# Key products of a gated recurrence computed on GpSimd instead of VectorE

## The reference, cut to what matters

```python
def hgrn2_chunked(q, log_f, v):
    ...
    def step(state, inp):
        qt, lf, vt = inp
        kt = -jnp.expm1(lf)
        cum = jnp.cumsum(lf, axis=2)
        diff = cum[:, :, :, None, :] - cum[:, :, None, :, :]
        decay = jnp.exp(jnp.where(causal[:, :, None], diff, -jnp.inf))
        attn = jnp.einsum('bhtd,bhsd,bhtsd->bhts', qt, kt, decay)
        o = attn @ vt + jnp.einsum('bhtd,bhde->bhte', qt * jnp.exp(cum), state)
        last = cum[:, :, -1:, :]
        state = jnp.exp(last[:, :, 0, :, None]) * state + jnp.einsum('bhsd,bhse->bhde', kt * jnp.exp(last - cum), vt)
        return state, o
```

## Time and profile before

| quantity | value |
|---|---|
| median of 3 runs | 4072.37 us (4066.07 to 4079.21) |
| profiled execution, its own time | 4077.13 us |
| its span in the trace | 4075.4 us |
| busy TensorE / VectorE / ScalarE | 3347.7 / 1556.2 / 897.1 us |
| busy GpSimd | 0.2 us |
| levels' loop, layer 0 | first decayed product at 317.0 us, last gather from 361.28 us |
| levels' loop, layer 1 | first decayed product at 1249.8 us, last gather from 1294.09 us |

### The profile page before, as it was taken

One profiled execution on the slowest core, in us unless ns is written; L12 is line 12 of the kernel. 1 busy time (PEld: TensorE's weight loads), 2 busy tenths in 40 slices (PEclk: granted clock), 3 DMA queues, 4 the chain that ended last, 5 costly groups with the idle time before them and its releaser, 6 DMA issues. The chain is left out here.

```text
span 4075.4 us, 38108 instructions
## 1 busy us (share of the span) xinstructions
PE 3347.7 (82%) x16560; PEld 2233.5 (55%) x16560; DVE 1556.2 (38%) x1877; ACT 897.1 (22%) x1359; POOL 0.2 (0%) x4
## 2 busy tenths in 40 slices
PE   5986779999886779998998756668788885888887
PEld 3665757886665766886455536554333353433332
DVE  3536626653636636662003445622111225211212
ACT  3433223223433213232104410120000021000001
POOL 0000000000000000000000000000000000000000
PEclk9995979999996879999998976779999997899999
DMA  6270012322262002322110390019989750798885
GB/s 219 83 245 25 1 31 87 100 83 81 77 204 86 1 31 73 96 96 94 52 62 11 103 310 1 29 56 391 391 325 378 306 187 21 275 386 355 342 346 213
DMA packets 321109, 637.04 MB, mean 156 GB/s; under 512 B 12848, under 2 KB 208432, under 8 KB 320816
## 3 DMA queue, kind: packets, MB, share of 16 engines
q1 hardware_dynamic: 317856, 627.22, 42.5%
q10 hardware_dynamic: 3088, 7.40, 0.5%
HBM read 632.48 MB, written 2.10 MB: 156 GB/s over the span
## 5 line engine op out<-in xcount | busy, mean ns | idle before, releaser
L524 PE MATMUL ps<-ring,work 128*64 128x512 f32 (+1 forms) x3584 | 583.3, 548 | 195.6 <-DMA ring<-in_w_mod 59.1
L524 PE MATMUL ps<-mix_halves,work_halves 128*128 128x512 f32 (+1 forms) x1456 | 587.7, 404 | 30.1 <-DVE h_halves L1779 30.0
L524 PE MATMUL ps<-h_halves,work_halves 128*128 128x512 f32 (+1 forms) x1456 | 574.4, 395 | 34.5 <-DVE mix_halves L1779 34.5
L524 PEld LDWEIGHTS ps<-ring,work 128*64 128x64 f32 (+1 forms) x3584 | 221.9, 137 | 544.1 <-issue 526.8
L524 PE MATMUL ps<-mix_halves,ring_halves 128*128 128x512 f32 x1264 | 495.7, 392 | 0.0
L1779 DVE TENSOR_TENSOR ring_halves<-ring,work_halves 128x2048 fp32r<-128x2048 f32 x108 | 239.1, 2214 | 320.2 <-ACT work_halves L1266 319.4
L524 PEld LDWEIGHTS ps<-mix_halves,work_halves 128*128 128x128 f32 (+1 forms) x1456 | 276.0, 190 | 111.8 <-issue 31.6
L524 PEld LDWEIGHTS ps<-h_halves,work_halves 128*128 128x128 f32 (+1 forms) x1456 | 276.8, 190 | 100.5 <-issue 43.6
L1266 ACT ACTIVATE work_halves<-ring 128x2048 fp32r<-128x2048 f32 x108 | 199.7, 1849 | 487.9 <-PE ps L524 391.7
L524 PEld LDWEIGHTS ps<-mix_halves,ring_halves 128*128 128x128 f32 x1264 | 238.2, 188 | 52.5
L524 PE MATMUL ps<-ring,proj 128*64 128x512 f32 x1024 | 237.6, 624 | 17.9 <-ACT proj L1637 15.6
(11 more groups left out here) (352 smaller groups left out, 3767.3 us busy)
## 6 DMA issues: line engine op xcount, KB each, us to landing
ring<-in_w_exp_gate SPq DMA_DIRECT2D x128, 1024.0 KB, 8.5
ring<-in_w_exp_up SPq DMA_DIRECT2D x128, 1024.0 KB, 13.0
ring<-in_w_exp_down SPq DMA_DIRECT2D x128, 1024.0 KB, 11.6
ring<-in_ada_w SPq DMA_DIRECT2D x48, 1024.0 KB, 11.0
ring<-in_w_mod SPq DMA_DIRECT2D x48, 1024.0 KB, 11.0
ring<-in_w_in SPq DMA_DIRECT2D x22, 1024.0 KB, 5.2
ring<-in_w_gate SPq DMA_DIRECT2D x22, 1024.0 KB, 5.4
ring<-in_w_up SPq DMA_DIRECT2D x22, 1024.0 KB, 5.3
```

Of the source, the lines that this page charges most:

```text
L524: i = pe.matmul(o, lhsT, rhs, start=start, stop=stop, **kw)
```

## The change

The product of k with `b_e` leaves VectorE's program. GpSimd gets a program: for every level of both layers it waits for `b_decay`, from level 3 on also for `b_score` (TensorE has read the buffer that it will overwrite), writes k times `b_e` to `b_k[n % 2]`, and gives the new signal `b_kk`. TensorE waits for `b_kk` beside `b_qk` before the scores of levels 1 to 7. ScalarE waits for `b_kk` before it starts on the next distances, since its exponential overwrites `b_e`, and once more behind the seven levels. VectorE's `b_qk` now comes from the query product alone. The texts of the signals' table are adapted.

```diff
@@ -760,6 +760,8 @@
                 chunk_turns(proj[:, 10:12, :], 2, 4, "b_v")
                 for n in range(len(LEVELS) + 1):
                     pe.wait_ge(*due("b_qk"))
+                    if n:
+                        pe.wait_ge(*due("b_kk"))
                     if n == 1:
                         pe.wait_ge(*due("b_v_sb"))
                     for hd in range(H1):
@@ -1436,9 +1438,12 @@
                 to("b_v_sb", f(b_vt, ps[:, 4:6, :].rearrange("p b (c f) -> p (b c) f", c=2), ACT.Copy))
                 for n in range(len(LEVELS)):
                     act.wait_ge(*due("b_diff"))
+                    if n:
+                        act.wait_ge(*due("b_kk"))
                     link(f(b_d, b_d, ACT.Abs))
                     to("b_decay", f(b_e, b_d, ACT.Exp, scale=-1.0))
                 act.wait_ge(*due("b_qd"))
+                act.wait_ge(*due("b_kk"))
                 link(f(b_e, b_cum, ACT.Exp))
                 to("b_decay", f(b_d, b_d, ACT.Exp, scale=-1.0))
                 link(f(stats[:, 32:40].rearrange("p (b c) -> p b c", b=2),
@@ -1721,6 +1726,19 @@
             act.wait_ge(sem["stored"], 16)
 
 
+        @block.gpsimd
+        def _(pool):
+            due = Due(sem)
+            for l in range(2):
+                due("b_score", H1)
+                for n in range(1, len(LEVELS) + 1):
+                    pool.wait_ge(*due("b_decay"))
+                    if n >= 3:
+                        pool.wait_ge(*due("b_score", H1))
+                    pool.tensor_tensor(b_k[n % 2], proj[:, 8:10, :], b_e, ALU.mult).then_inc(sem["b_kk"], 1)
+                due("b_decay")
+                due("b_score", 2 * H1)
+
         @block.vector
         def _(dve):
             due = Due(sem)
@@ -1933,8 +1951,7 @@
                 difference(LEVELS[0])
                 for n in range(1, len(LEVELS) + 1):
                     dve.wait_ge(*due("b_decay"))
-                    tt(b_q[n % 2], q, b_e, ALU.mult)
-                    to("b_qk", tt(b_k[n % 2], z, b_e, ALU.mult))
+                    to("b_qk", tt(b_q[n % 2], q, b_e, ALU.mult))
                     dve.wait_ge(*due("b_qk", 2 if n == 1 else 1))
                     if n < len(LEVELS):
                         difference(LEVELS[n])
```

More of the change, by code:

```diff
@@ L220 @@
     "b_z": "VectorE: clamped logits", "b_ez": "ScalarE: exp(-z)", "b_f": "VectorE: forget gates", "b_lf": "ScalarE: their logs",
-    "b_qk": "VectorE: a level's q and k", "b_score": "TensorE: a head's scores", "b_acc": "VectorE: taken where they hold",
+    "b_qk": "VectorE: a level's q", "b_kk": "GpSimd: a level's k", "b_score": "TensorE: a head's scores", "b_acc": "VectorE: taken where they hold",
     "b_diff": "VectorE: distance to the level's middle", "b_decay": "ScalarE: its decay", "b_qd": "VectorE: distance to the chunk's end",
```

## The result

The changed kernel takes 4090.36 us (median of 13 runs, 4081.0 to 4095.22) where the kernel before, run beside it, takes 4076.28 (13 runs, 4066.07 to 4080.71). The ratio is 1.0034 with a 95% interval of 1.0024 to 1.0043, so +14 us with bounds of about +10 and +18. 4090 was forecast.

The account below looks back on a forecast made before the run. VectorE was taken to set the pace, 6.13 us a level. Twelve periods at +1.28 us (+15.4) and two last levels (+2.6) sum to +18.0; from the median 4072.37 the forecast is 4090 us, range 4058 to 4108.

Parts of the forecast that it names:

- Taking turns: VectorE's two-SBUF-input products and GpSimd's key product can't overlap: level 7.41 us, +18.0 in all; chance 0.57.
- together: Opposite case at the levels' start: both engines' products run at the same time, level about 5.15 us, sum -11.7.
- the marks named in advance: Profile signs in the levels: late or stretched distances (about 3.7 us), level 7.4 us, gathers 0.72, VectorE idle or stretched.
- that sum: A level's period: query product 1.23, GpSimd 2.45, to the gather 1.14, to the next level 2.59; 7.41 us.
- The term for G: Duration of GpSimd's 128x1024 key product, not in the earlier trace: taken as 2.45 us, bounds 1.22 and 6.55.
- Together and fast: First rival: both products overlap in the levels, GpSimd's under 3.7 us; 4060.7 us; chance 0.26 for under 3.
- Together with a slow GpSimd: Second rival: products overlap, but ScalarE's loop sets the pace; 4066 to 4079 us, at most 4112; chance within a shared 0.08.
- Turns with a slow GpSimd: Third rival: no overlap in the levels and GpSimd's product at 3.3 us, +30, 4102 us; chance 0.09 for over 3.
- No real change: Fourth rival: TensorE's start doesn't move, GpSimd's product at 1.22 us, +0.7 in all; chance within a shared 0.08.
- the cheaper order: In a level, distances slip in before GpSimd's product: +1.01 us a period, +14.7 in all.

Follow-up runs that it names:

- the query from PSUM: Changed kernel, but from level 2 on VectorE's query product reads a PSUM bank in place of q; 4078.5 us, one run (kernel before: 4070.91).
- the product beside the gather: Changed kernel, but GpSimd starts its key product only after query product and distances, ScalarE waiting before its exponential; 4076.24 us, ratio to before 1.0005.

## Why the prediction was right, and where it was off

**The mechanism.** Taking turns was the step that decided the sign, and it came out. From rows it was chosen against "together" by one comparison, 692 ns for a one-input operation and 1218 for a two-input one, read as VectorE having no read capacity left over for GpSimd. The comparison doesn't carry that, and the trace of the kernel before had the rows against it:

```profile
L2392 DVE TENSOR_TENSOR work<-proj,ps 128x1024 f32<-128x1024 f32 x16 | 19.5, 1221 | 186.5 <-PE ps L524 186.5
...
L1840 DVE TENSOR_REDUCE small<-h 128x4 f32<-128x1024 f32 x16 | 19.5, 1220 | 0.5
```

A product with only one input in SBUF takes 1221 ns and a reduction of a single input 1220, the same as two SBUF inputs. So a row's length doesn't tell how many read paths it takes, and as far as the sign rested on this comparison it was luck. What shows it are the runs: VectorE stretched with two SBUF inputs, not with one, and not against a write.

Of the marks named in advance, these came out: gathers at 0.72, a level over 6.13, TensorE late in the last level, and a stretched VectorE row with no idle time. Which row was named wrongly: the distances were to wait or to be stretched to 3.7 us; it was the query product, at 3.16, in six levels of seven, and the distances, at 3.25, in the first alone. The level was to be 7.4 us and is 6.93.

**The size.** A level was put at 7.41 us and is 6.93, so +0.80 where +1.28 was forecast. Three terms of that sum were off. GpSimd's product takes 2.34 us and not 2.45 (0.11). GpSimd starts at the decay while VectorE is still in its gather, so 0.27 us of its time lie beside work that doesn't collide; I let it start behind the query product, though the earlier trace rows had the room, 0.33 us between the exponential's end and VectorE's. And a product that has been held ends 1.08 us after the release, where I had put 1.23 for it (0.15). Together 0.53, less 0.05 for the steps between rows that the sum had left out: 0.48. That the order of the two hardly matters, as I wrote, is right to 0.1 us: the first level, where VectorE went ahead, costs 0.88 (6.93 against 6.05). For twelve levels (the first two of a layer cost 0.9 each) and the two last ones (+0.82 and +0.14 instead of +1.29 each; in layer 1 TensorE's last scores took 4.39 us instead of 5.13, at a mean granted clock of 0.78 from 1300 to 1310 us, between its two levels, against 0.50 before, the lower one, 1.2 GHz) the sum is 10.9 in the loops against 18.0 forecast.

**The total.** 4090 against 4090.36 looks closer than the working deserves. I added 18.0 to a median of 3 runs, 4072.37; 13 runs gave 4076.28 for the same kernel. The change measured is 14 us, with an interval that contains 10.9 and ends at 17.5; the forecast's +18 is just above it. So the loss was forecast two thirds too large by the loops, some 30% by the medians, and a start that was 4 us too low hid it. That the two errors cancel to 0.4 us is luck.

**The term for G.** The ratio of the memsets (2.03) and twice VectorE's time (2.45) stand on both sides of 2.34. The estimate from the Trainium skill's figure (GPSIMD Engine Reference, "Elementwise — side-by-side cycle accounting"), 4497 ns halved to 2.25 us, is 0.09 short of the measured 2.34.

**The rivals.** Together and fast: 128x1024 reads of GpSimd do run at full speed beside VectorE, but only beside one SBUF input (the gathers, and the query from PSUM). What it would have brought with GpSimd at 2.34 us no run shows; with a GpSimd product of 0.20 us the loops gain 17, where the forecast had 14 for one of 1.22 us. Together with a slow GpSimd, so that ScalarE's wait for `b_kk` is the loop: wrong here, but it is much what the product beside the gather became at 6.33 us a level. Turns with a slow GpSimd: its product takes 2.34 us, far from the 3.3 that this needed. No real change, with GpSimd's product at 1.22 in the key product's old place: neither that duration nor a level of 6.18 came, and TensorE's start moved by 0.82 us. What the forecast called the cheaper order, distances ahead of GpSimd, never happened: where GpSimd had been held it went ahead of the distances that were issued after it.

## What to carry to other kernels

In these runs a GpSimd product cost VectorE nothing beside instructions that had one of their two inputs in PSUM; beside those with both inputs in SBUF VectorE waited until GpSimd was through, which cost 1.94 us a level for a product of 2.34. The product that VectorE was spared is worth 1.13 us, so the offload lost. Look for the stretch of VectorE's program that reads PSUM (here the gather, 2.56 us), start GpSimd's work by the signal of the last two-input instruction ahead of it, and give the tile that it reads a second buffer, or the engine that overwrites it becomes the loop. And when such a collision is suspected, look for longer rows and not for waits: it appears as busy time.

## What the runs showed that I had not expected

- The profile's row of a held instruction contains the wait: GpSimd's 3.38 us are 1.04 of waiting and 2.34 of work, VectorE's 3.16 are 2.08 and 1.08. The engine's busy time goes up, and its idle time doesn't.
- The hold is by instruction and first come first served: a GpSimd product of 128x8, 0.20 us by itself, took 1.24 behind a query product that had started 0.04 us earlier.
- A held two-input product of 128x1024 ends 1.08 us after the release, not 1.22; a part of its usual time lies in the wait.
- A GpSimd memset of 128x1024 takes 0.95 us and disturbs nothing, whether it starts 0.03 us into VectorE's product or 0.2 us ahead of it.
- TensorE's scores of a level, the same 16 matmuls, took 2.79, 4.39 or 5.13 us in the last level of different kernels, by the granted clock. A kernel whose end hangs on them can gain or lose up to 2.3 us a layer that its edit didn't ask for.
- GpSimd's product beside the gather, with four semaphores waited for ahead of it, starts 0.23 us after the row of the last signal's instruction (337.00 + 1.23 to 338.46). In the changed kernel, with two, it started 0.07 us after ScalarE's row (326.82 + 1.06 to 327.95). What of this is the number of waits and what the engine that signals, no run tells apart.
